# Out-projection inside an RWKV stage: three of four column groups as seven block products

## What is computed

```python
proj = rms_norm(x, norm_mix) @ w_in
y_s5, y_lru, y_rw, y_ssd = s5_mixer(...), rglru_mixer(...), rwkv7_mixer(...), ssd_mixer(...)
mixed = concatenate([y_s5, y_lru, y_rw, y_ssd], axis=-1)      # 512 x 2048
x = x + mixed @ w_out                                         # w_out 2048 x 2048
h = rms_norm(x, norm_ffn)
x = x + hier_moe(h, ...)                                      # 64 experts, 2 for each token
out = rms_norm(x, norm_final)
```

## Time and profile before

| | |
|---|---|
| time, median of 3 runs | 2404.32 us (2401.41 to 2405.39) |
| profiled execution, its own time | 2401.06 us |
| its span | 2398.8 us, 33897 instructions |
| PE busy | 2225.1 us, 93% |
| PEld busy | 1248.6 us, 52% |
| DVE, ACT, POOL busy | 788.0, 448.3, 401.1 us |
| DMA | 760.83 MB, mean 317 GB/s |

### The profile page before, as it was taken

How to read it: one execution, slowest core, us unless ns; L and a number is a source line. 1 busy time by engine, 2 the same in 40 slices (tenths; PEclk the granted TensorE clock), 3 DMA queues, 4 the chain that set the end, 5 groups by cost and what they waited for, 6 DMA issues and landing times.

```text
span 2398.8 us, 33897 instructions
## 1 busy us (share of the span) xinstructions
PE 2225.1 (93%) x13339; PEld 1248.6 (52%) x13339; DVE 788.0 (33%) x1289; ACT 448.3 (19%) x788; POOL 401.1 (17%) x589
## 2 busy tenths in 40 slices
PE   8999999999999999999998888898888888888887
PEld 4577778885555456444444444344443444434443
DVE  6799684356333314111111111111111111111114
ACT  3544352115222221000000000000000000000002
POOL 4022223331422001111111111101011111111110
PEclk9999999999999999999999999999999999999999
DMA  6588869873321466999999999999999999999998
GB/s 191 115 171 181 184 135 215 168 162 108 99 81 56 141 272 258 411 428 424 426 427 424 427 426 425 428 425 426 428 424 429 425 426 427 425 426 427 424 426 366
DMA packets 237801, 760.83 MB, mean 317 GB/s; under 512 B 36024, under 2 KB 173564, under 8 KB 193948
## 3 DMA queue, kind: packets, MB, share of 16 engines
q1 hardware_dynamic: 174008, 710.29, 73.9%
q0 software_dynamic: 54016, 42.00, 9.7%
q10 hardware_dynamic: 9700, 7.45, 1.0%
HBM read 753.23 MB, written 47.19 MB: 334 GB/s over the span
## 4 chain that ended last, share of the span: by engine, by line
PE 50%; DMA 42%; DVE 7%; issue 1%; ACT 0%; ACTq 0%; DVEq 0%; SPq 0%; POOL 0%; POOLq 0%
DMA big<-in_moe_w 40%; PE ps L3045 12%; PE ps L2689 11%; PE ps L2756 7%; PE ps L3076 4%; DVE big L1546 3%; PE ps L2656 3%; PE ps L2922 2%; DMA big<-in_norm_final 1%; PE ps L3061 1%; PE ps L2843 1%; PE ps L3029 1%; PE ps L2823 1%; PE ps L2704 1%; DVE big L1700 1%
## 5 line engine op out<-in xcount | busy, mean ns | idle before, releaser
L3045 PE MATMUL ps<-big 128*64 128x384 f32 x4096 | 697.1, 495 | 93.8 <-DMA big<-in_moe_w 83.6
L3045 PEld LDWEIGHTS ps<-big 128*64 128x64 f32 x4096 | 298.7, 139 | 498.5 <-issue 364.7
L3076 PE MATMUL ps<-big 128*64 128x512 f32 x1536 | 390.9, 664 | 51.0 <-DVE big L2378 51.0
L2689 PE MATMUL ps<-big 128*128 128x256 f32 x1792 | 393.8, 380 | 2.6 <-DVE big L1678 2.6
L2689 PEld LDWEIGHTS ps<-big 128*128 128x128 f32 x1792 | 338.6, 190 | 60.5 <-issue 12.5
L2374 DVE TENSOR_SCALAR big<-ps,scal 128x384 f32<-128x384 f32 x64 | 39.6, 618 | 690.8 <-PE ps L3045 690.8
L3076 PEld LDWEIGHTS ps<-big 128*64 128x64 f32 x1536 | 115.5, 151 | 279.5 <-issue 219.0
L2383 DVE SCALAR_TENSOR_TENSOR big<-ps,scal,big 128x512 f32<-128x512 f32 x128 | 90.2, 747 | 397.8 <-PE ps L3076 397.8
L1463 ACT ACTIVATE big<-ps,scal 128x384 f32<-128x384 f32 x64 | 37.2, 581 | 793.7 <-PE ps L3045 769.0
L1033 POOL COPY scal<-slots 128x3 f32 (+1 forms) x64 | 11.9, 187 | 907.4 <-DVE big L2383 892.1
L2756 PE MATMUL ps<-big 128*128 128x512 f32 x320 | 153.5, 610 | 0.9 <-ACT big L1216 0.7
(11 more groups left out here) (446 smaller groups left out, 1780.8 us busy)
## 6 DMA issues: line engine op xcount, KB each, us to landing
big<-in_moe_w SPq DMA_DIRECT2D x187, 3072.0 KB, 38.4
big<-in_w_in SPq DMA_DIRECT2D x96, 512.0 KB, 4.8
big<-in_w_in POOLq DMA_DIRECT2D x32, 512.0 KB, 7.9
big<-big POOLq DMA_DIRECT2D x16, 512.0 KB, 5.1
big<-in_w_out SPq DMA_DIRECT2D x8, 1024.0 KB, 5.5
big<-y_rows SPq DMA_DIRECT2D x8, 1024.0 KB, 27.9
big<-in_moe_w SPq DMA_DIRECT2D x4, 1536.0 KB, 23.4
big<-in_x SPq DMA_DIRECT2D x4, 1024.0 KB, 8.4
```

Source lines behind the costliest of these rows:

```text
L2689: last = nc.tensor.matmul(o, w[:, k, :], side[:, k, :], start=(k == 0 and b in (0, 1, 5)), stop=(k == 7), skip_group_check=True)
L3045: last = nc.tensor.matmul(ps[2 + w][B * g:B * g + B, 0:FF], xT[k][:, j, B * g:B * g + B], W13[k][w][:, NJ * g + j, :], start=(j == 0), sto ...
L3076: last = nc.tensor.matmul(ps[5 + q][B * g:B * g + B, :], hid[k][:, m, :], W2[k][:, m, 512 * n:512 * n + 512], start=(m == 0), stop=(m == F ...
```

## The change

The 1536 rows of `w_out` and the 512 tokens are cut in two halves each, and the columns go in four groups `g` of twice 256 (`1024 n + 256 g`). Each group is then a 2x2 by 2x2 block product. Group 0 stays plain: eight block products, each 256 tokens by 256 columns over 768 rows. Groups 1 to 3 are done with seven block products, by sums of token blocks (`OT1` to `OT4`, formed once by POOL in `sides` and DVE in `last_side`) and sums of weight blocks (formed by POOL's accumulating DMAs in `accumulate`). The products of a group add up in banks 6 and 7, and DVE adds or subtracts the state of a bank to a quarter of `x` after each of the seven (`out_part` on DVE). A block `m` (29 of them, `OB`) is 12 matmuls of 256 columns. Weights go through four slots of 768 KB. ACT's copies and POOL's adds of the pieces are gone, and the gate product of the RWKV part (`lora` with index 2, four matmuls of 512 columns, before at line 2771 ahead of the first piece) is moved behind `mean`. The first lines show the tiles, then the order and the shares, SP's part, POOL's, DVE's and PE's:

```diff
+        wo_slot = [big[:, 62:65, :].rearrange("p a n -> p (a n)"), big[:, 65:68, :].rearrange("p a n -> p (a n)"), small[:, 0:1536],
+                   big[:, 68:71, :].rearrange("p a n -> p (a n)")]
+        wo_slot = [x.rearrange("p (c n) -> p c n", c=6) for x in wo_slot]
...
+        mix_in = [[Y5[:, 0:2], Y5[:, 2:4], YL[:, 0:2]], [YL[:, 2:4], Z_[:, 0:2], Z_[:, 2:4]]]
+        O11, O12, O21, O22 = ([x[:, :, TO * t:TO * t + TO] for x in mix_in[k]] for k in range(2) for t in range(2))
+        OT1 = [two(big[:, i, :]) for i in (92, 93, 94)]
+        OT2 = [two(big[:, i, :]) for i in (16, 17, 19)]
+        OT3 = O12
+        OT4 = [two(big[:, 95, :]), two(big[:, 56, :])]
+        OT4_LAST = [small[:, 1536:1792], big[:, 18, 256:512]]
+
+        def wo_side(b, c):
+
+            if b == 6 and c >= 4:
+                return OT4_LAST[c - 4]
+            return (O11, OT1, OT2, O22, OT3, O21, OT4)[b][c // 2][:, c % 2]
...
-        for m in range(16):
-            plan(("po", m), m if m < 2 else 7)
+        OB = [(0, 0)] * 8 + [(g, b) for g in range(1, 4) for b in (5, 0, 1, 2, 3, 4, 6)]
+        OB_AT = {x: m for m, x in enumerate(OB)}
+        OB_LAST = {1: 0, 3: 2, 5: 1, 7: 3}
+        for g in range(1, 4):
+            for q, bs in enumerate(((5, 0), (6,), (2, 3), (1, 4))):
+                OB_LAST[max(OB_AT[g, b] for b in bs)] = q
+        OB_PAIRS = 20
+        NOB = len(OB)
+        OB_W = [0, 1, 0, 1, 2, 3, 2, 3] + list(range(4, NOB - 4))
+        OB_TO = {5: (0, 0, 1), 0: (0, 0, 1), 1: (1, 1, -1), 2: (1, 0, 1), 3: (1, 0, 1), 4: (1, 1, -1), 6: (0, 1, -1)}
+        OB_SUM = {0: ["A11"], 1: ["A22", "A21"], 2: ["A11", "S1"], 3: ["A12", "S2"], 4: ["A21", "A11"], 5: ["A12"], 6: ["A22"]}
+
+        def ob_sum(w):
+
+            return [("A11", "A12", "A21", "A22")[w]] if w < 4 else OB_SUM[OB[w + 4][1]]
+
+        for m, (g, b) in enumerate(OB):
+            if g:
+                plan(("po", m), 7 if b % 2 == 0 else 6)
+            elif m % 2:
+                plan(("po", m), 6 if m % 4 == 3 else 7)
...
-        share = [(("prep", 0), 6), (("prep", 1), 6), (("prep", 2), 12)]
-        sizes = itertools.cycle([1, 5, 4] + [2, 2] * (LEV - 1))
+        share = [(("prep", 0), 12), (("prep", 1), 12), (("prep", 2), 24)]
+        sizes = itertools.cycle([2, 10, 6] + [4, 2] * (LEV - 1))
         for c0 in range(0, NRC, 2):
             share += [(where, next(sizes)) for where in [("pre", c0), ("pre", c0 + 1), ("t", c0, 0)]
                       + [(x, c0, lv) for lv in range(1, LEV) for x in ("t", "u")]]
-        share += [(("chain", c, step), 3) for c in (NRC - 2, NRC - 1) for step in range(3)]
-        share += [(("mean",), 6), (("var",), 24)]
+        share += [(("chain", c, step), 6) for c in (NRC - 2, NRC - 1) for step in range(3)]
+        share += [(("mean",), 24), (("var",), 48)]
...
+            def piece(m):
+
+                g, b = OB[m]
+                if ("po", m) in at:
+                    k, i = at["po", m]
+                    sp.wait_ge(full[k], i + 1)
+                elif m == 6:
+                    sp.wait_ge(wo_free, WO_FREE + 1)
+                for w in {3: (4, 5), 6: (6,), 7: (7,)}.get(m, (m,) if 8 <= m < NW else ()):
+                    wo_load(w)
+                if OB_PAIRS <= m < OB_PAIRS + 4:
+                    c = m - OB_PAIRS
+                    if c == 0:
+                        sp.wait_ge(ro_ok, NRC - 2)
+                    sp.dma_start(wo_rw[:, c, :], wov[:, 8 + c, :]).then_inc(x2b_in, 16)
+                if m - 1 in OB_LAST and OB[m - 1][0] < 3:
+                    x_load(OB_LAST[m - 1], OB[m - 1][0] + 1)
+                if m in OB_LAST and m != NOB - 1:
+                    q = OB_LAST[m]
+                    sp.wait_ge(free[k], i + 1)
+                    sp.dma_start(x_quad(q, g, x2d), xpart[q].rearrange("p (i c) -> p i c", i=2)).then_inc(x_io[q], 16)
...
+            def accumulate(w):
+
+                g, b = OB[w + 4]
+                name = ob_sum(w)[1]
+                done, z = WO_IN[w][1]
+                pool.wait_ge(*WO_IN[w][0])
+                pool.wait_ge(done, z - 16)
+                if name[0] == "S":
+                    n = OB_AT[g, int(name[1])] - 4
+                    pool.wait_ge(*WO_IN[n][-1])
+                    nc.gpsimd.dma_start(wo_slot[w % 4], wo_slot[n % 4], accum_op=ALU.add).then_inc(done, 16)
+                else:
+                    wo_plain(pool, w, name, nc.gpsimd.dma_start, done, accum_op=ALU.add)
+
+            def sides(c0, lv):
+
+                if (c0, lv) == (0, 1):
+                    for c in range(3):
+                        side_op(OT1[c], O11[c], O12[c], sub, 1 if c == 2 else False)
+                if (c0, lv) == (0, 2):
+                    for c in range(3):
+                        side_op(OT2[c], O12[c], O22[c], sub)
+                    g.settle()
+                if (c0, lv) == (0, 3):
+                    for c in range(3):
+                        side_op(OT2[c], OT2[c], O11[c], sub, 2 if c == 2 else False)
+                if (c0, lv) == (2, 1):
+                    b, i = at[("po", 7)]
+                    pool.wait_ge(full[b], i + 1)
+                    for c in range(3):
+                        side_op(OT3[c], O22[c], OT3[c], sub, 3 if c == 2 else False)
...
+            def out_part(where):
+
+                for m in ends[where]:
+                    g, b = OB[m]
+                    if g:
+                        t, n, sign = OB_TO[b]
+                        q = 2 * t + n
+                    elif m in OB_LAST:
+                        q, sign = OB_LAST[m], 1
+                    else:
+                        continue
+                    src, done = got(("po", m))
+                    dve.wait_ge(x_io[q], X_AT[g])
+                    to, a, z = xpart[q], src[:], xpart[q]
+                    if m == NOB - 1:
+                        dve.wait_ge(ro_ok, NRC)
+                        to = big[:, 40:48, :].rearrange("p a n -> p (a n)").rearrange("p (i d) -> p i d", i=2)[:, :, 1792:2048]
+                        a, z = (x.rearrange("p (i c) -> p i c", i=2) for x in (a, z))
+                    v.tell(nc.vector.scalar_tensor_tensor(out=to, in0=a, scalar=float(sign), in1=z, op0=MUL, op1=ADD), *done)
+                    v.settle()
+
+            def last_side():
+
+                dve.wait_ge(padd_ok, 2)
+                for c in range(2):
+                    v.do(nc.vector.scalar_tensor_tensor(out=OT4[c], in0=OT2[c], scalar=-1.0, in1=O21[c], op0=MUL, op1=SUB))
+                for c in range(2):
+                    ins = nc.vector.scalar_tensor_tensor(out=OT4_LAST[c], in0=OT2[2][:, c], scalar=-1.0, in1=O21[2][:, c], op0=MUL, op1=SUB)
+                    if c == 0:
+                        v.do(ins)
+                v.tell(ins, side_ok, SIDES + 2)
+                v.settle()
...
+                    m, r = divmod(at_, PO)
+                    i, c = divmod(r, 6)
+                    g, b = OB[m]
+                    fresh = b in (0, 1, 5) if g else m % 2 == 0
+                    o, k = at[("po", m if g else m // 2 * 2 + 1)]
+                    if r == 0:
+                        if m == 0:
+                            pe.wait_ge(mix_ok, 12)
+                            pe.wait_ge(away_in, AWAY_IN + 32)
+                        if g or fresh:
+                            pe.wait_ge(free[o], k)
+                        pe.wait_ge(*wo_summed(m))
+                        if g == 1 and b in (1, 2, 4):
+                            pe.wait_ge(padd_ok, {1: 1, 2: 2, 4: 3}[b])
+                        if g == 1 and b == 6:
+                            pe.wait_ge(side_ok, SIDES + 2)
+                    side = wo_side(b, c) if g else (O11, O21, O12, O22)[m % 4][c // 2][:, c % 2]
+                    last = nc.tensor.matmul(ps[o][:, TO * i:TO * i + TO], side[:, P * i:P * i + P], wo_slot[OB_W[m] % 4][:, c, :],
+                                            start=(r == 0 and fresh), stop=(c == 5), skip_group_check=True)
+                    if r == PO - 1:
+                        if ("po", m) in at:
+                            last.then_inc(full[o], 1)
+                        elif m == 6:
+                            last.then_inc(wo_free, 1)
...
+            pe.wait_ge(gates_in, 48 + 64)
+            for q in range(WT):
+                o, done = fill(("lora", q, 2))
+                nc.tensor.matmul(o[:], loraG[:, P * q:P * q + P], LO[:, 1, :], start=True, stop=True).then_inc(done, 1)
             blocks64("var", mixd, cen_ok)
```

287 lines of the change are left out of this document (148 added, 139 removed).

## The result

The changed kernel takes 2410.05 us (median of 17 runs, 2406.35 to 2416.45) against 2402.69 us (17 runs) for the kernel before beside it: a ratio of 1.0030, 95% interval 1.0023 to 1.0038. A second comparison gave 1.0028 (1.0019 to 1.0037). So it is some 7 us slower, where the forecast had 1.7 us less. The time lies inside the forecast's range, at the end where rival C stood. The 17 runs of the kernel before also lie 1.6 us under the median of three from which the forecast started. The profiled execution of the changed kernel took 2406.76 us, its span is 2405.0.

What follows compares the result with a forecast made beforehand. The RWKV stage was taken as bound by PE's own work; -2.0 + 3.5 - 20.0 + 0.1 + 0.5 + 2.1 + 12.4 + 1.7 = -1.7 us gave 2402.6 us, range 2395.5 to 2411.

Steps and rivals of the forecast that it cites:

- rival C: Chunk pairs: POOL's queue of accumulating transfers lands late and PE waits; +8 us, 2410.6 us in all; 17%.
- The filler's saving: Four chunk pairs: fewer filler matmul columns make each pair 5.0 us shorter, 20.0 us in all.
- The start: Ahead of the first rw_pre: the gate product is moved away, but DVE's last product limits the gain; -2.0 us.
- The wait behind the first gram: Pair 0: PE waits for DVE to add up bank 7 behind the masks of chunk 0; +3.5 us.
- that in the chain: Chain: block 21 waits for DVE to add block 20 in bank 7, behind rw_state; +2.1 us.
- those in the tail: Tail, mean to out_rw: 3.9 us idle ahead of block 27, about 1 ahead of block 28; tail +12.4 us.
- I put 0.5 us for all of this: Chunk pairs: the smaller filler still covers the levels' waits and DVE's adds fit; 0.5 us for small waits.
- I count one fall: PE's clock: falls once, behind the longer idle stretch, in the tail; +1.7 us.
- its upper case: PE's clock: two falls, one behind each long idle stretch; 1.7 us more than with one.
- B: Faster: clock stays up (-1.7), small waits don't show (-0.5), fixed cost of a run falls (-3); 2397.4 us; 28%.
- A: The forecast itself: 20 us saved in the pairs, given back in the tail and two waits; 2402.6 us; 47%.
- D: Chunk pairs: levels become bound by latency with the small filler, 0.5 us lost in each; +10, 2412.6 us; 8%.

Runs made afterwards that it cites:

- run 3: Changed kernel with POOL's OT3 subtractions moved two levels later, from level 1 to level 3 of the second pair: 2404.98 us, 1.0008 of the kernel before.
- run 4: Changed kernel with all weight transfers from the fifth slot on, plain and accumulating, thinned to a sixth (stale weights): 2402.72 us, 1.0003 of the kernel before.
- run 7: Changed kernel with only POOL's accumulating transfers thinned to one of six row blocks (incomplete weights): 2403.14 us, 0.9998 of the kernel before.
- run 8: Changed kernel with only the plain weight transfers from the fifth slot on thinned to one of six row blocks: 2406.89 us, 1.0019 of the kernel before.
- run 2: Changed kernel with the first pair's 12 filler matmuls moved behind the second chunk's rw_pre: 2405.67 us, 1.0012 of the kernel before.
- run 11: Changed kernel with six more 256-column matmuls ahead of block 26 to keep PE busy in the tail's wait (output differs): 2408.79 us, 1.0026 of the kernel before.
- run 6: Changed kernel with the edits of run 1, run 2 and run 3, and the chain's adds ahead of the state update: 2398.41 us, 0.9984 of the kernel before.
- run 1: Changed kernel with DVE adding block 25 ahead of the layer norm instead of behind it: 2405.38 us, 1.0012 of the kernel before.
- run 10: The four edits of run 6 once more, unchanged: 2397.58 us (9 runs), 0.9973 of the kernel before.
- run 5: The changed kernel once more, without further edits, as a control: 2408.64 us, 1.0028 of the kernel before.
- run 9: Run 6's four edits, plus the weight sum for block 27 counted on another semaphore: 2394.37 us (5 runs), 0.9964 of the kernel before.

## Why the prediction was wrong

**Right.** The filler's saving: pairs 2 and 3 without their stops, and pair 1 in run 3 with 42.1 us, give the 5.0 us for each pair. The start gained 2.9 us, not 2.0, since DVE's product also came earlier. The wait behind the first gram was 3.33 us (3.5 forecast), that in the chain 1.75 (2.1), those in the tail 3.10 and 0.84 (3.9 and 1.0), and the tail in all 48.2 (48.3 with the clock). That the tail agrees to 0.1 us is in part luck: the two waits were 1.0 us shorter, and its products together 0.8 longer. The norm's last products took 2.5 us where 2.8 was taken. The mechanisms of these terms held, and the reorderings that rest on them gave what they should in the trace.

**Wrong: "I put 0.5 us for all of this", the step on the pairs.** It was mis-sized by some 8 us, and by two things it did not have. First, the wait: I set DVE's operations at their old durations and gave POOL's twelve subtractions as a mere replacement of its adds. Three of them stretched one DVE subtraction from 0.42 to 3.29 us, 2.9 us more at a place with 0.4 to spare: 2.48 us of wait, and in some executions a slow clock behind it. Moving them removed it (run 3). Secondly, the traffic: I took the levels for safe because every engine had time to spare and the bus was "nearly idle here", and looked only at who waits for a weight or a sum. PE also waits for its own instructions, which come by DMA. The new transfers make it stop in the midst of rows of small matmuls, 4.8 us in all, with some 0.2 us more at each start. That the weight transfers cause these stops is shown (runs 4, 7 and 8), and the packets below show how.

**Wrong: "I count one fall", the clock.** There were two, in pair 0 and in the tail. The forecast had the second as its upper case at 1.7 us; it measured 1.6 by run 2. Of the other profiled executions with 3.3 us there only that of run 4 kept full clock. The rule that I weighed there (the Trainium skill, TensorE: Matmul & The Clock Gate, section HAM oscillation — how this bites in real kernels: bursts with long waits between them start each time on the slow clock) was the better count, and the trace agrees with it at both places.

**The forecast's sum, mended:** out of 8.2 us between 838.7 and 846.9, pair 0 has 1.9 (clock 1.6, a DVE wait 0.35), pair 1 has 5.0 (2.5 of DVE wait, 1.7 of stops, the rest at their starts and in small waits), pairs 2 and 3 have 3.2 (3.1 of stops), against -0.9 at the start, -0.5 in the chain, -0.1 in the tail and the 0.5 allowed.

**The rivals.** B's lower fixed cost of a run hardly showed: pair 2 without a stop took 42.2 us in run 4, 0.2 less than A has, where B wants some 0.6 in each. D fell: beyond the one stretched operation the levels waited for DVE twice, 0.35 and 0.27 us, and never for ACT. C named the right transfers and a wrong effect. They landed in 6.6 to 9.6 us, below the 11 from which `OF` would have been late, and no `rw_t` of the changed kernel waited for POOL (in run 11 one did, for 0.61 us in pair 3). But the time was near C's 2410.6, by what the transfers do to PE's stream in the pairs; in the tail the row of sums that C describes lay hidden behind the wait on the norm. That the time came out near C's is thus no success of C's mechanism.

**What the stops are.** They have no releaser. But the profile has a queue "q8 instruction" with packets of 16 KB, and the packet records of the traces tie it to PE's stream and to the stops. First, the places: counted in matmul records the stops lie whole multiples of 125 to 126 apart (records 3575, 3701, 3951, 4704, 4830, 5206 and 5332), and 3319 records pass between 600 and 800 us beside 26 such packets, 3093 beside 24 before. So a packet goes with some 126 records and the instructions between them. Secondly, each of the 36 stops of this stretch, in all profiled executions and with the one of 0.32 us in the kernel before, ends 1.2 to 1.6 us after the latest packet has landed. The stop of 2.04 us in run 3, for one, begins at 720.42. One packet starts within 0.1 us behind 720.0 (this row is the window from 720 to 721):

```profile
q8 instruction: 1, 0.02, 5.8%
```

5.8% of 16 engines in 1 us is 0.93 us, so it lands at 721.0, inside the stop, and PE goes on at 722.46. Thirdly, the stop is as long as the packet is late. At this place (record 4830, near 725 us), with the packet's start counted from when PE passed the place before, some 125 records earlier:

| execution | packet starts after, us | stop, us |
|---|---|---|
| run 4, both thin | 0.45 | none |
| run 8, plain thin | 0.44 | none |
| run 6 | 2.17 | 0.56 |
| run 1 | 2.45 | 0.84 |
| run 7, sums thin | 2.58 | 0.82 |
| changed | 3.28 | 1.49 |
| run 3 | 3.75 | 2.04 |
| run 10 | 4.19 | 2.31 |

The other four (runs 2, 5, 9 and 11) lie between 2.35 and 3.37 us, with stops of 0.49 to 1.49. So PE stops because its next instructions come late, and they start late beside the weight transfers. Run 4 has the same instructions on PE without any stop, so their number alone is not the cause.

**Open.** Why a packet starts up to 4.2 us late at this place, whether it waits in the DMA engines behind the weights' packets or is asked for late, is not shown. No run changed PE's instructions alone. Nor was it tried whether the sums could be formed in another way than by accumulating transfers.

## What to carry to other kernels

Before calling work on GpSimd free, list the DVE instructions beside it that read both operands from SBUF, and put it where none of them is on the path; one with an operand in PSUM is no such case. A wait is worth what stands behind it: look for the second releaser that the named one covers (here a sum that landed almost as late), and count the clock behind each long idle stretch (here 3.1 and 3.3 us), not behind one of them. Extra transfers were not free here, though no engine waited for their data: they made PE's instruction packets late. Where PE runs many small matmuls beside heavy traffic, look at stops without a releaser and at the instruction queue's packets ahead of them. An edit that saves 5 us of PE time for each pair and adds half as many bytes again paid only once its waits were mended (0.9964 with five small edits); the stops stayed.

## What was not expected of the hardware

- PE stopped for 0.2 to 2.3 us within rows of matmuls that wait for no semaphore, at a few fixed instructions in nearly every execution, beside accumulating and many small-packet transfers. Each stop ended 1.2 to 1.6 us after a packet of 16 KB of the instruction queue had landed. With the weight transfers thinned to a sixth there was none from 600 to 800 us.
- An accumulating transfer of 768 KB took 6.6 to 9.6 us to land in the pairs and up to 11.8 in the tail.
- One DVE subtraction of 128x256 with both operands in SBUF took 3.29 us beside POOL's subtractions, against 0.42 with those moved (run 3); an operation with one operand in PSUM kept its 0.69 us beside the same ones.
- The granted clock fell behind idle stretches of 2.85 us and more in 16 of 17 cases, behind the stops of 2.03, 2.04, 2.16 and 2.31 us too (8 records in 3.49 to 3.66 us instead of 1.99), but not behind one of 1.89 or a wait of 2.56 us, and behind the wait of 2.48 us in some executions and not in others. In the tail the fall cost 1.6 to 3.2 us.
